# One table set for logarithm and exponential on ScalarE, and one exponential moved, in a two-layer hybrid decoder step

## What is computed

```python
proj = x @ w_in                                   # 1024 x 4112
qkv_c = silu(causal_dwconv(qkv, conv_buf, conv_w))
q = l2_normalize(q) * (GDN_DK ** -0.5);  k = l2_normalize(k)      # x * rsqrt(sum x^2 + eps)
g = -exp(a_log) * softplus(a + dt_bias);  beta = sigmoid(b)
gcum = cumsum(g, axis=-1)                         # within a chunk
decay_mask = exp(where(tril, diff, -inf))
rhs = concatenate([vb, kb * exp(gcum)[..., None]])
...                                               # triangular solve, chunk by chunk
o = o * rsqrt(mean(o * o) + eps) * norm_w * silu(z);  y = o @ w_out
```

## Time and profile before

| what | value |
|---|---|
| median of 3 runs | 1611.09 us (1609.63 to 1611.42) |
| the profiled execution, its own time | 1608.85 us |
| its span | 1607.1 us |
| PE busy | 1566.4 us, 97% |
| DVE busy | 1287.6 us, 80% |
| ACT busy | 1052.1 us, 65% |
| expert loop and end | from about 610 us on |

### The profile page before, as it was taken

How to read it: one execution, slowest core, us unless ns; L and a number is a source line. 1 busy time by engine, 2 the same in 40 slices (tenths; PEclk the granted TensorE clock), 3 DMA queues, 4 the chain that set the end, 5 groups by cost and what they waited for, 6 DMA issues and landing times.

```text
span 1607.1 us, 23697 instructions
## 1 busy us (share of the span) xinstructions
PE 1566.4 (97%) x8974; PEld 1358.5 (85%) x8974; DVE 1287.6 (80%) x1295; ACT 1052.1 (65%) x963; POOL 103.7 (6%) x155
## 2 busy tenths in 40 slices
PE   7999999999999999999999999999999999999995
PEld 7899989999999997888888888888888888888883
DVE  5886545688447868889889889889889889889897
ACT  5974334676335445777778777777777778777772
POOL 3105000011000011000000000000000000003100
PEclk9999999999999999999999999999999999999998
DMA  9737604598556538999999999999999999999991
GB/s 276 247 125 260 243 2 154 190 296 302 178 168 199 180 114 285 380 368 369 381 366 370 381 364 372 380 369 363 384 369 363 383 370 365 382 368 365 391 398 45
DMA packets 227446, 476.66 MB, mean 297 GB/s; under 512 B 9692, under 2 KB 69100, under 8 KB 227081
## 3 DMA queue, kind: packets, MB, share of 16 engines
q1 hardware_dynamic: 216040, 435.66, 76.0%
q0 software_dynamic: 11344, 40.12, 7.4%
HBM read 449.74 MB, written 26.24 MB: 296 GB/s over the span
## 4 chain that ended last, share of the span: by engine, by line
PE 91%; ACT 4%; DVE 3%; issue 1%; DMA 0%; DVEq 0%; SPq 0%; ACTq 0%
PE bank L2091 13%; PE bank L2088 13%; PE bank L2087 13%; PE bank L2116 13%; PE bank L385 11%; PE bank L2122 6%; PE bank L391 5%; PE bank L1958 2%; PE bank L2099 2%; PE bank L1784 1%; PE bank L1805 1%; PE bank L1963 1%; PE bank L1802 1%; ACT high L345 1%; PE bank L396 1%
## 5 line engine op out<-in xcount | busy, mean ns | idle before, releaser
L350 DVE TENSOR_TENSOR low<-raw,high 128x2048 fp32r<-128x2048 f32 x405 | 923.3, 2289 | 171.3 <-ACT high L345 170.9
L345 ACT ACTIVATE high<-raw 128x2048 fp32r<-128x2048 f32 x405 | 775.2, 1917 | 312.4 <-PE bank L2091 105.4
L2087 PE MATMUL bank<-high,xgh 128*128 128x512 f32 x896 | 359.9, 402 | 0.6 <-DVE xgl L1518 0.6
L2088 PE MATMUL bank<-high,xgl 128*128 128x512 f32 x896 | 356.2, 398 | 0.0
L2091 PE MATMUL bank<-low,xgh 128*128 128x512 f32 x896 | 247.7, 398 | 3.4 <-DVE low L350 3.4
L2091 PEld LDWEIGHTS bank<-low,xgh 128*128 128x128 f32 x896 | 169.1, 190 | 47.3 <-DVE low L350 6.8
L2087 PEld LDWEIGHTS bank<-high,xgh 128*128 128x128 f32 x896 | 169.3, 189 | 39.4 <-issue 1.0
L2088 PEld LDWEIGHTS bank<-high,xgl 128*128 128x128 f32 x896 | 169.2, 189 | 38.9
L385 PE MATMUL bank<-xhb,high 128*128 128x266 f32 (+1 forms) x752 | 158.6, 293 | 1.8 <-DVE utail L1114 1.8
L385 PE MATMUL bank<-xlb,high 128*128 128x266 f32 (+1 forms) x752 | 155.8, 289 | 0.0
L2116 PE MATMUL bank<-high,hth 128*128 128x512 f32 x448 | 140.6, 395 | 0.0
(11 more groups left out here) (414 smaller groups left out, 1602.3 us busy)
## 6 DMA issues: line engine op xcount, KB each, us to landing
raw<-in_moe_w_gu_dram SPq DMA_DIRECT2D x224, 1024.0 KB, 5.5
raw<-in_moe_w_down_dram SPq DMA_DIRECT2D x112, 1024.0 KB, 5.4
raw<-in_ffn_w_gu_dram SPq DMA_DIRECT2D x22, 1024.0 KB, 5.9
raw<-in_gdn_w_in_dram SPq DMA_DIRECT2D x16, 1024.0 KB, 12.3
tok<-zeros POOLq DMA_DIRECT2D x26, 512.0 KB, 18.1
raw<-in_sc_w_in_dram SPq DMA_DIRECT2D x12, 1024.0 KB, 5.4
raw<-in_ffn_w_down_dram SPq DMA_DIRECT2D x11, 1024.0 KB, 5.1
s<-in_state_gdn_S_dram POOLq DMA_DIRECT2D x8, 512.0 KB, 7.1
```

The costliest lines, as they stand in the source:

```text
L345: eng.activation(high[:, n % SPLIT, :], raw[:, n % RAW, :], ACT.Copy).then_inc(high_ready, 1)
L350: eng.tensor_tensor(low[:, n % RAW, :], raw[:, n % RAW, :], high[:, n % SPLIT, :].bitcast(F32), ALU.subtract).then_inc(low_ready, 1)
L2087: pe.matmul(out, xgh[:, 4 * kh + k, :], wh[:, k, :], start=kh + k == 0, stop=False)
L2088: pe.matmul(out, xgl[:, 4 * kh + k, :], wh[:, k, :], start=False, stop=False)
```

## The change

In every place where a set with the logarithm alone was loaded, the set that holds both logarithm and exponential is loaded. An explicit load of that set is put ahead of the first Exp in iteration 1. The load behind the output's squares (L840) is taken out, since nothing displaces the joint set there. The exponential of `nbe` moves from iteration 4 to the end of iteration 5, behind group 1's Exp, and VectorE's use of it from iteration 5 to iteration 7.

```diff
                 if n == 1:
+                    act.preload_act_table_set("natural_log_exp_and_others")
                     act.wait_ge(gate_a, 1)
...
-                    act.wait_ge(gcol_ready, 1)
-                    act.activation(nbe[:, :, :], gcol[:, :, 0, :], ACT.Exp).then_inc(nbe_ready, 1)
                 if n in (2, 4, 6, 8):
...
                 if n in (3, 5, 7, 9):
                     g = (n - 3) // 2
-                    act.preload_act_table_set("natural_log")
+                    act.preload_act_table_set("natural_log_exp_and_others")
...
                     act.activation(squares[:, :, :], squares[:, :, :], ACT.Exp, scale=-0.5).then_inc(sq_inv, 1)
+                    if n == 5:
+                        act.wait_ge(gcol_ready, 1)
+                        act.activation(nbe[:, :, :], gcol[:, :, 0, :], ACT.Exp).then_inc(nbe_ready, 1)
...
             act.activation(zgate[:, :, :], zgate[:, :, :], ACT.Silu).then_inc(z_ready, 1)
-            act.preload_act_table_set("natural_log")
+            act.preload_act_table_set("natural_log_exp_and_others")
...
             out_squares(1)
-            act.preload_act_table_set("natural_log")
...
             def norm_scale(l):
-                act.preload_act_table_set("natural_log")
+                act.preload_act_table_set("natural_log_exp_and_others")
...
             expert(final, True)
-            act.preload_act_table_set("natural_log")
+            act.preload_act_table_set("natural_log_exp_and_others")
...
                 if n == 5:
-                    dve.wait_ge(nbe_ready, 1)
-                    step(dve.scalar_tensor_tensor(nbe[:, :, :], nbe[:, :, :], -1.0, gcol[:, :, 1, :], ALU.mult, ALU.mult))
                     dve.wait_ge(gate_in, 64)
                     dve.wait_ge(gcol_ready, 1)
                     decay_exponent(0)
+                if n == 7:
+                    dve.wait_ge(nbe_ready, 1)
+                    step(dve.scalar_tensor_tensor(nbe[:, :, :], nbe[:, :, :], -1.0, gcol[:, :, 1, :], ALU.mult, ALU.mult))
```

## The result

The changed kernel takes 1601.2 us in the median of five runs (1600.07 to 1604.9), beside 1611.09 us before (1608.37 to 1611.42). The ratio is 0.9945, with a 95% interval from 0.993 to 0.996: 0.55% faster, 8.9 us, between 6.4 and 11.3 (the medians themselves lie 9.9 us apart). The forecast was 6.3 us faster, 1604.8.

The account below looks back on a forecast made before the run. PE was taken as the bound, so removed ScalarE loads count only where PE waits. Projection waits 3.8, clock 1.7, mixer's end 0.65 + 0.18 make 6.3 us: 1611.1 - 6.3 = 1604.8 us, range 1601.9 to 1608.3.

Parts of the forecast that it names:

- group 1's wait: Input projection, iteration 4: PE's wait for group 1's squares shrinks from 1.71 to 0.37 us, held by gcol; gain 1.34 us.
- group 2's wait: Input projection, iterations 5 and 6: PE's wait for group 2's squares goes; gain 1.32 us.
- group 3's wait: Input projection, iterations 7 and 8: PE's wait for group 3's squares shrinks from 1.88 to 0.7 us; gain 1.17 us.
- clock behind group 3: PE's fall to half clock at 95.5 to 97.0 us, behind the third wait, goes; gain 1.7 us, lower bound 0.
- L1828's wait: End of the mixer: wait for the copies at L815 falls from 1.41 to 0.8 us without the load at L810; gain 0.65 us.
- end of the mixer: Two waits of PE there, for the copies and at L1876: gains 0.65 and 0.18 us, bounds 0.4 and 1.6.
- last LayerNorm's load: Load at L1006, 1594.50 to 1595.78 us, lies beside L1641, which runs to 1597.92; costed at nothing.
- rate of Exp in the joint set: Slower rival: Exp and Ln from the joint set run slower; at double, 4 us slower, 1615 us; chance 0.03.
- the first step: Iterations 1 to 4: removing the load at L725, ahead of group 0's squares, moves nothing on PE; 0 us.
- The clock as a term: First rival: clock stays low or falls elsewhere, 4.6 us, 1606.5, chance 0.12; with a second fall 2.9 us, 1608.2, chance 0.06.
- VectorE did not take ScalarE's place: Second rival: VectorE becomes the limit up to slot 12 of the projection; total gain 5.1 us, 1606.0 us; chance 0.09.
- The case of a price of 2.7 us a load: Fourth rival, the ceiling: removed loads are worth more and PE stops waiting altogether; 8.2 us, 1602.9 us; chance 0.06.

Follow-up runs that it names:

- nbe_only: Kernel before, with only the exponential of the write strength moved and the separate sets kept (two loads fewer): 1606.9 us, ratio 0.9979.
- pairs_only: Kernel before, with the joint set in iterations 3, 5, 7 and 9 alone (four loads fewer): 1607.18 against 1609.64 us, ratio 0.9981.
- tail_only: Kernel before, with the joint set only in the mixer's end (five loads fewer): 1611.64 against 1610.2 us, ratio 1.0004.
- no_first: Changed kernel without the explicit joint load in iteration 1: 1602.31 us against 1610.2 for the kernel before, ratio 0.9952.
- after_again: Changed kernel, unchanged, run and profiled once more: 1600.08 us, ratio 0.9932 to the kernel before.
- extra_load: Changed kernel with one load of the set already loaded added ahead of group 3's squares: 1603.85 us, ratio 0.9966 to the kernel before.
- the last version: Changed kernel with beta's Sigmoid replaced by Exp and a reciprocal, and gcol copied earlier: 1598.67 us, ratio 0.9933; repeated 1602.11, ratio 0.9956.
- first_only: Kernel before, with only the joint set loaded ahead of iteration 1's first Exp (one load fewer): 1607.37 against 1610.2 us, ratio 0.9981.
- fill: Kernel before, no load removed, small products queued on PE ahead of the waits for groups 0 to 3's squares: 1607.49 against 1609.64 us, ratio 0.9982.

## Why the prediction was right, and where its size was off

**Right: which waits, and what is late next.** For each step, the forecast and the trace of after:

| step | forecast | measured |
|---|---|---|
| group 1's wait | 0.37, for gcol | 0.33, for gcol (L1126) |
| group 2's wait | none | none |
| group 3's wait | 0.7 | 0.81 |
| clock behind group 3 | full, 1.7 us | full, 7.58 - 5.97 = 1.61 us |
| L1828's wait | 0.8 | 0.78 |
| end of the mixer | 0.83 us | 163.70 - 162.66 = 1.04 us |
| last LayerNorm's load | nothing | L2156 to the end of the span 23.2 us in both |
| rate of Exp in the joint set | as before | 1.06 us |

From group 0 to slot 12 the two first traces differ by 65.15 - 59.79 = 5.36 us, and with the mixer's end 6.4 us. The sum of the forecast, 6.3, is this.

**Mis-sized: the first step.** "What goes before it (the load at L725, group 0's load at L757) moves nothing on PE" was wrong for L725. I took L709's wait of 0.21 us for PE at slot 4 as a sign that ScalarE no longer mattered. But PE comes to slot 4 behind group 0's sums, and these need ScalarE's squares. In the profiled execution the squares ended at 46.98 us and the sums began at 47.35: ScalarE had been 0.3 us short of holding PE, and that margin was there only because PE had lost time at slot 2. In the other six traces with the load it held PE. The term was 0 and measured 47.35 - 46.04 = 1.31 us between the first traces: 0.99 because the squares ended earlier (1.28 for the load, less 0.29 for a later start of ScalarE's stretch), and 0.32 because PE had no wait at slot 2 this time, which is the execution's. Against the ordinary execution of before it is larger, 47.80 - 46.04 = 1.76 us plus 1.56 for the clock behind group 0 (17.06 us to group 1 instead of 15.50). The run with this load alone gave 3.1 us (1.6 to 4.5).

**Mis-sized: the clock.** I priced one fall, the one that the profiled execution showed behind group 3. Six traces keep the load at L725 and the group 0 as it was, or nearly: both of before, nbe_only, pairs_only, tail_only and no_first. In five of them there is another fall, behind waits of 2.5 to 3.2 us at group 0, and the first trace of before has its own at slot 2 instead. So behind the first term there stood a second fall of some 1.6 us that the forecast did not have.

**Not in the forecast, and in part chance.** Of the 9.0 us between the two spans, 1.31 + 5.36 + 1.04 = 7.7 are the steps above and 1.3 arose behind the second LayerNorm. That stretch, from the second LayerNorm to the last products, took 1096.2 to 1104.8 us in thirteen profiled executions, and not in the order of the kernels: 1100.5 and 1100.9 before, 1099.2 and 1104.0 after. What differs is how long the clock stays low at the router. The window at the router in the first trace of the changed kernel, and behind it in the second:

```profile
580.00:610.00 30.00, 28.09 (x156) 0.94 0.55 200
```

```profile
580.00:610.00 30.00, 30.00 (x121) 0.54 0.26 101
```

This makes the medians spread by several microseconds. It is not the execution's alone. The three traces with a low clock of over 20 us there (after_again, tail_only, extra_load) have mean clocks of 0.985 to 0.987. Of the 59 runs of the kernel before that stood beside the experiments none is under 0.989; of the 85 runs of the changed and edited kernels 15 are at 0.987 or less, seven of them tail_only's, three the last version's. So how often it happens depends on the kernel too. What in it decides was not tried.

The accounts meet: the second LayerNorm stands at 484.4 us in the mean of the two traces of before, at 475.4 in the mean of the two after, 9.0 us (the two traces of before are themselves 2.0 us apart), and the two ratios of the change give 8.9 and 10.9 us.

**The rivals.** The clock as a term was the right doubt, and it went the other way: more came back, not less. VectorE did not take ScalarE's place at slot 12 (no such wait in the traces of the changed kernel, where the samples' keys were ready at 104.48 + 0.20 = 104.68 for a start at 105.83, 1.15 us before against the 0.9 worked out), though 0.3 us of exactly that wait (L396 for kS) shows in first_only and in fill. The case of a price of 2.7 us a load gave 1602.9 and lies nearest to the median, for a wrong reason: a load costs 1.29 us on the path.

## What to carry to other kernels

Two engines that meet within a few tenths of a microsecond are one bound, and the profile may show a wait for neither: before costing an edit at nothing because "PE was already late", look back to what put PE there. Profile the kernel before twice where the terms are a microsecond or two, since one execution can hide a wait that all the others have. And look behind a wait of PE of some 2 us for what the clock does there: where it fell, as in this kernel, shortening the wait paid twice, and so did filling it.

## What was not expected of the hardware

**Short waits and the clock.** Of the waits of PE between 28 and 125 us in the thirteen traces, those up to 1.77 us had no low clock behind them; those of 2.5 us and more (2.51, 2.74, 3.07, 3.17, 3.19) all had; of those between, six had one (1.80, 1.85, 1.88 twice, 2.03, 2.11) and three had none (1.82, 2.09, 2.10). The clock fell from 2.4 to 1.2 GHz for about 3 us each time, and cost about 1.6 us.

**A low clock under a busy engine.** In the second trace of the changed kernel PE was busy for 30.0 of 30.0 us at the router with a mean clock of 0.54. Work without a gap did not bring the clock back there for over 20 us.
